# The reciprocal square roots of all norms, as one power on GpSimd in place of a root on ScalarE and a reciprocal on VectorE

## What is computed

```python
def _rmsnorm(x, g):
    xf = x.astype(jnp.float32)
    y = xf * lax.rsqrt(jnp.mean(xf * xf, axis=-1, keepdims=True) + NORM_EPS)
    return (y * g.astype(jnp.float32)).astype(x.dtype)
# layer one
h = _rmsnorm(x, p['ln_pre_a'][i]) * (1.0 + scale[:, None, :]) + shift[:, None, :]
...
x = x + gate[:, None, :] * _rmsnorm(y, p['ln_post_a'][i])
# between the layers and in layer two: the same two norms, and one per head
o = (_rmsnorm(o, p['subln_b'][j]) * (1.0 - lambda_init)).astype(x.dtype)
y = jnp.dot(o.reshape(b, t, DA_WIDTH) * jax.nn.silu(g), p['w_out_b'][j])
x = x + gate[:, None, :] * _rmsnorm(y, p['ln_post_b'][j])
```

## Time and profile before

| what | value |
|---|---|
| median of 3 runs | 1000.04 us |
| the runs | 1000.96, 994.45, 1000.04 us |
| span of the profiled execution | 1000.7 us |
| instructions in it | 15785 |
| busy: TensorE, VectorE, ScalarE, GpSimd | 914.8, 478.4, 414.2, 69.1 us |
| mean granted TensorE clock | 0.965 |

### The profile page before, as it was taken

One profiled execution on the slowest core, in us unless ns is written; L12 is line 12 of the kernel. 1 busy time (PEld: TensorE's weight loads), 2 busy tenths in 40 slices (PEclk: granted clock), 3 DMA queues, 4 the chain that ended last, 5 costly groups with the idle time before them and its releaser, 6 DMA issues.

```text
span 1000.7 us, 15785 instructions
## 1 busy us (share of the span) xinstructions
PE 914.8 (91%) x5704; PEld 700.9 (70%) x5704; DVE 478.4 (48%) x844; ACT 414.2 (41%) x889; POOL 69.1 (7%) x121
## 2 busy tenths in 40 slices
PE   2999999989999999889895899999989999888895
PEld 1576666767667777655684788888868888766784
DVE  0543232212277777466634824252366565456924
ACT  3421212102166656455626622242255555446623
POOL 0000000000111110021003000000010000110002
PEclk8799999989989999999898899999999999999999
DMA  9845654655410103197323122434201101488422
GB/s 340 322 166 187 233 196 142 209 212 189 126 43 22 42 21 126 57 328 258 137 84 134 38 101 74 180 108 145 64 22 43 40 23 43 149 296 268 171 85 105
DMA packets 71716, 138.35 MB, mean 138 GB/s; under 512 B 4592, under 2 KB 22256, under 8 KB 71536
## 3 DMA queue, kind: packets, MB, share of 16 engines
q1 hardware_dynamic: 68976, 127.15, 37.5%
q0 software_dynamic: 2688, 10.49, 2.7%
HBM read 121.37 MB, written 16.25 MB: 138 GB/s over the span
## 4 chain that ended last, share of the span: by engine, by line
PE 82%; DMA 5%; DVE 4%; ACT 4%; issue 3%; SPq 2%; POOL 0%; DVEq 0%; ACTq 0%
PE bank L1528 18%; PE bank L1530 18%; PE bank L1529 18%; PE bank L1831 3%; PE bank L1692 3%; PE bank L1587 3%; PE bank L1569 2%; PE bank L1743 2%; PE bank L1709 2%; PE bank L1700 2%; PE bank L1846 2%; DMA arena<-in_mod_w_a 2%; PE bank L1542 1%; PE bank L1754 1%; PE bank L1792 1%
## 5 line engine op out<-in xcount | busy, mean ns | idle before, releaser
L1528 PE MATMUL bank<-w_parts,h_parts 128*128 128x512 f32 x640 | 257.7, 403 | 7.2 <-DVE h_parts L1111 3.6
L1530 PE MATMUL bank<-w_parts,h_parts 128*128 128x512 f32 x640 | 251.7, 393 | 0.0
L1529 PE MATMUL bank<-w_parts,h_parts 128*128 128x512 f32 x640 | 251.4, 393 | 0.0
L719 ACT ACTIVATE w_parts<-arena 128x1024 fp32r<-128x1024 f32 x64 | 67.4, 1054 | 213.2 <-PE bank L1530 200.1
L1528 PEld LDWEIGHTS bank<-w_parts,h_parts 128*128 128x128 f32 x640 | 121.6, 190 | 44.5 <-issue 14.1
L1105 DVE TENSOR_TENSOR w_parts<-arena,w_parts 128x1024 fp32r<-128x1024 f32 x64 | 78.2, 1222 | 129.8 <-ACT w_parts L719 129.4
L1530 PEld LDWEIGHTS bank<-w_parts,h_parts 128*128 128x128 f32 x640 | 121.4, 190 | 26.4
L1529 PEld LDWEIGHTS bank<-w_parts,h_parts 128*128 128x128 f32 x640 | 121.7, 190 | 23.7
L1528 PE MATMUL bank<-h_parts,w_parts 128*128 128x320 f32 x256 | 90.0, 351 | 0.8 <-ACT arena L809 0.8
L1530 PE MATMUL bank<-h_parts,w_parts 128*128 128x320 f32 x256 | 79.4, 310 | 0.0
L1529 PE MATMUL bank<-h_parts,w_parts 128*128 128x320 f32 x256 | 79.3, 310 | 0.0
(11 more groups left out here) (159 smaller groups left out, 1237.6 us busy)
## 6 DMA issues: line engine op xcount, KB each, us to landing
arena<-in_w_in_a SPq DMA_DIRECT2D x32, 512.0 KB, 5.8
arena<-in_mod_w_b SPq DMA_DIRECT2D x24, 512.0 KB, 4.7
arena<-in_mod_w_a SPq DMA_DIRECT2D x4, 2048.0 KB, 15.6
arena<-in_mod_w_kv SPq DMA_DIRECT2D x16, 512.0 KB, 5.2
arena<-in_cache_a_k SPq DMA_DIRECT2D x8, 1024.0 KB, 7.0
arena<-in_cache_a_v SPq DMA_DIRECT2D x8, 1024.0 KB, 6.4
arena<-in_w_kv_b SPq DMA_DIRECT2D x16, 512.0 KB, 3.5
arena<-in_w_in_b SPq DMA_DIRECT2D x16, 512.0 KB, 3.8
```

Of the source, the lines that this page charges most:

```text
L719: nc.scalar.activation(whl[:, n % 2, 0, :], wraw[n % 2], ACT.Copy).then_inc(s_whi, 1)
L1528: mm(out, ah, wh, start=start, stop=False)
L1529: mm(out, ah, wl, start=False, stop=False)
L1530: return mm(out, al, wh, start=False, stop=stop)
```

## The change

One function `root` on GpSimd raises a variance to the power of -0.5 (`tensor_tensor` with `ALU.pow` against a tile `minus_half`, filled once at the start). It takes the place of ScalarE's Sqrt and VectorE's reciprocal at all 14 places: two of 128x5, ten of 128x1, one of 128x32, one of 128x8. The semaphores `sqrt_done` and `y_sqrt` are gone. GpSimd waits for the variance and signals "ready" itself. In the residual updates GpSimd's list is now root 0, root 1, addition 0, root 2, addition 1, and so on.

```diff
+        minus_half = sb("minus_half", [P, NT * PAIRS])
...
+            def root(dst, src, n):
+                return nc.gpsimd.tensor_tensor(dst, src, minus_half[:, 0:n], ALU.pow)
+
+            def norm_root(stage):
+                a, b = TT * stage, TT * (stage + 1)
+                pool.wait_ge(s_var, stage + 1)
+                root(rstd[:, a:b], ss[:, a:b], TT).then_inc(s_rstd, 1)
+                pool.wait_ge(s_rstd, stage + 1)
+
+            nc.gpsimd.memset(minus_half[:, :], -0.5).then_inc(s_half, 1)
+            pool.wait_ge(s_half, 1)
+            norm_root(0)
             store("ak", knat, 1)
...
                 for t in range(TT):
-                    pool.wait_ge(s_ys, layer * TT + t + 1)
-                    nc.gpsimd.tensor_tensor(x[:, t, 0:NC], x[:, t, 0:NC], ysb[:, t, 0:NC], ALU.add).then_inc(s_x2p, 1)
+                    pool.wait_ge(s_yv, layer * TT + t + 1)
+                    root(yvar[:, 0, t:t + 1], yvar[:, 1, t:t + 1], 1).then_inc(s_yr, 1)
+                    pool.wait_ge(s_yr, layer * TT + t + 1)
+                    if t == 0:
+                        continue
+                    add_y(layer, t - 1)
+                add_y(layer, NT)
                 pool.wait_ge(s_x2p, (layer + 1) * TT)
...
             residual(0)
+            norm_root(1)
...
+            pool.wait_ge(s_ov, 1)
+            root(osum[:, 0:NT * PAIRS], osum[:, 0:NT * PAIRS], NT * PAIRS).then_inc(s_osr, 1)
+            pool.wait_ge(s_ov, 2)
+            pool.wait_ge(s_osr, 1)
+            root(osum[:, NT * PAIRS:], osum[:, NT * PAIRS:], PAIRS).then_inc(s_osr, 1)
+            pool.wait_ge(s_osr, 2)
             residual(1)
...
-                act.wait_ge(s_var, stage + 1)
-                nc.scalar.activation(ss[:, TT * stage:TT * (stage + 1)], ss[:, TT * stage:TT * (stage + 1)],
-                                     ACT.Sqrt).then_inc(s_sqrt, 1)
...
-            def y_root(layer, t):
-                act.wait_ge(s_yv, layer * TT + t + 1)
-                nc.scalar.activation(yvar[:, 2, t:t + 1], yvar[:, 1, t:t + 1], ACT.Sqrt).then_inc(s_ysr, 1)
...
-            def head_root(columns, n):
-                act.wait_ge(s_ov, n)
-                nc.scalar.activation(osum[:, columns], osum[:, columns], ACT.Sqrt).then_inc(s_osr, 1)
...
-                dve.wait_ge(s_sqrt, stage + 1)
-                nc.vector.reciprocal(rstd[:, a:b], ss[:, a:b]).then_inc(s_rstd, 1)
...
-                dve.wait_ge(s_ysr, layer * TT + t + 1)
-                nc.vector.reciprocal(yvar[:, 0, t:t + 1], yvar[:, 2, t:t + 1]).then_inc(s_yr, 1)
...
-                link(nc.vector.reciprocal(osum[:, c], osum[:, c]))
```

## The result

The changed kernel took 1015.28 us (median of 4 runs, 1013.93 to 1016.77), beside 1000.5 us for the kernel before: a ratio of 1.0147, 95% interval 1.0109 to 1.0184. The forecast was 1000.9 with a range up to 1009. So the change costs 10 to 15 us. The places at which it acts lose 9.1 to 9.3 us in both traces of the changed kernel. What else the first set has stays open.

What follows compares the result with a forecast made beforehand. It took the kernel to be bound by TensorE's matmuls, which the change leaves alone. Gains of 2.4 us less 3.3 us of powers made a net loss of 0.9 on 1000.04: 1000.9 us, range 994 to 1009.

Steps and rivals of the forecast that it cites:

- the price of a power: Each GpSimd power: 0.2 us fixed plus 0.04 us a column, estimated from additions; 1.48 us for 128x32.
- 6 p1 + p5 + p32: Powers counted on the path, p1, p5, p32 being durations of 128x1, 128x5, 128x32 (0.24, 0.40, 1.48 us): 3.3 us.
- Rival (1): Power slow per column on GpSimd: chance 0.13 beyond 0.25 us a column (over 10 us), 0.04 from 0.1 to 0.25.
- 43 c - 0.8: Net loss in us if a power costs c us a column; passes 10 us from c = 0.25.
- Place A: First norm: comes 1.3 - p5 earlier, but TensorE's modulation and transposes cap the gain; 0.25 us taken.
- Place B: Residual update after `ya` and second norm: 1.1 - 3 p1 earlier at the square sums, 0.3 - p5 at the norm.
- Place C: Head norms: prompt 0.57 - p32 earlier; the samples' 128x8 power has 2.2 us and costs nothing.
- Place D: Last residual update, no table load there: 0.2 - 3 p1 earlier, a loss with any p1 above 0.07 us.
- Rival (2): First GpSimd power waits for code to load; a delay of 5 us gives 1005 us; chance 0.05.
- Rival (3): All removed loads, roots and reciprocals lie on the path: 6.8 us gained, 993 us; chance 0.03.
- The rule on table loads: ScalarE: the trace shows a 1.28 us load without the skill's further 1380 ns drain, which would add 1.4 us gain.
- Next to nothing lies around: Whole kernel: the profiled span of 1000.7 us was set 0.7 above the median of 1000.04.

Runs made afterwards that it cites:

- the first set: First four runs of the changed kernel beside the kernel before: median 1015.28 us, ratio 1.0147.
- delay: Kernel before with 13 chained small VectorE instructions, 2.7 us together, ahead of the second norm's variance: 1005.18 us, ratio 1.0033.
- best of both: Kernel before with the Sqrt table loaded ahead of the updates and the head norms' roots as split GpSimd powers: 1000.83 us, ratio 0.9991.
- price kernel: Kernel before with a row of powers and additions of several widths on scratch tiles while GpSimd is idle: 1001.09 us (one run).
- the second: Second set of four runs of the unaltered changed kernel, against the kernel before at 1001.23 us: 1010.8 us, ratio 1.0096.
- the repetition: Changed kernel, unaltered, run and traced again beside the kernel before: 1010.8 us, ratio 1.0096.

## Why the prediction was wrong, point by point

**What fails is the price of a power.** The step reads: "I take twenty additions, 0.04 us a column", on a fixed part of 0.2 us. Measured alone it is 0.157 us a column and 0.39 fixed. The term 6 p1 + p5 + p32 was put at 3.3 us. With the durations of the changed kernel's trace it is 6 x 0.99 + 1.18 + 5.46 = 12.6, and the same sum then gives a loss of 10.2 us in place of 0.9.

Of the 9.3 us between the two losses, 5.0 come from the slope, 1.5 from the fixed part and 2.7 from a third thing that the price left out: six of the powers stand in GpSimd's queue beside VectorE's updates and take 0.99 us, not the 0.55 of one alone. The slope was chosen between 0.002 and 1.3 without a row near it, from twenty steps of a routine; what the routine is, no run shows. The prediction named its own sign of being wrong, a 128x32 row above 5 us, and that came: 5.46.

That the sum with the right durations, 10.2, comes near the 9.1 to 9.3 of the traces is in part luck. It has the two updates 1.2 and 1.0 us too dear, and it lacks 1.0 us behind the second norm and the 0.25 at the first that never came. It has no term for the fall of the clock either. Rival (1) had the right mechanism, a routine per column. But its formula, 43 c - 0.8, gives 6 us at c = 0.157, since it has 0.2 us of fixed part for each of the eight powers, and the six of 128x1 take 0.99, not 0.36. The range ended at c = 0.25 on that formula, and so ended too low.

**Place A**: "It can save at most 1.90 - 1.64 = 0.26. Taken: 0.25, which holds while p5 is below 1.0." p5 was 1.18, and nothing was gained. Right by its own condition.

**Place B**: the 0.7 us at the first addition came about as predicted, 0.8 (3.23 against 4.06 us). "1.1 - 3 p1" would have been a loss of 1.9 with p1 = 0.99; measured 0.7. Two things made the difference. The additions were put at 1.43 us, but ahead of a power they take 1.26 to 1.29 (0.5 us for three). And the waits and gaps were put at 0.47 us, but one instruction follows the other in GpSimd's list within 0.02 us (0.4 us). That the longer mean of before holds time in which an addition waited for VectorE, which now falls on the powers, is a likely reading and not tested. The next norm's square sums, foretold 0.4 us earlier, start later. "0.3 - p5" gives a loss of 0.88; measured 0.86.

**An overlooked cover.** "Behind this norm's root on GpSimd are queued only the clears of `qz` and the stores of K and V, which nobody needs for a long time." Nobody needs them, but the root holds them back until VectorE scales. Then both slow down: 3.12 us for 2.08, 3.55 for 2.25. Between scaling and the store of K, the six traces with that overlap (the changed kernel twice, heads and updates put back, powers earlier, heads split) lose 0.98 to 1.77 us, 1.35 in the mean. The four without it (norms put back, clears moved, delay, best of both) lose 0.02 to 0.48, 0.30 in the mean. That is 1 us more.

**Place C**: "0.57 - p32" with 5.46 gives 4.89; measured 4.82, and 0.00 with the roots put back. For the samples, "The power of 128x8 has 2.2 us and costs nothing": it took 2.02 us, and VectorE waits for a head power only once, for the large one. Right.

**Place D**: "0.2 - 3 p1" gives a loss of 2.8; measured 1.7, for the same two reasons: the five additions take 6.8 us in place of 7.16, and the steps between 0.1 in place of 0.7.

**Rival (2)**, that the first power waits for code: it took 1.19 us, the second 1.18. In the price kernel the configuration instructions stand at 194.7 us and the first power starts at 194.85, with 0.56 us. Neither shows a delay. The slack of place A was put at 1.0 us; with p5 = 0.40 it is 0.9, and it holds the 0.25 that was already counted as gained. The 6 us that the Trainium skill has for a first call (GPSIMD Engine Reference, "Instruction dispatch") are not seen here. **Rival (3)** fell with the sum.

**The rule on table loads.** By the Trainium skill (ScalarE: Activation LUTs, "What ACT_TABLE_LOAD costs"), with its further 1380 ns of drain, place B would have been better by another 1.4 us. It isn't: the third square starts 1.36 us behind the second now (536.14 to 537.50), where it was 2.11, a gain of 0.75. Load and root together took 1.40 us (536.13 to 537.53), and the square now waits 0.67 us for TensorE in their place; that leaves no room for a drain.

**"Next to nothing lies around"** the span was wrong: the executions here take 1.75 to 1.87 us more than their spans (1016.77 against 1014.9; 997.66 against 995.9). The sum doesn't hang on it, since both kernels have it.

**What stays open.** Why the first set of the changed kernel has a median 4.5 us above the second. The one trace of it that there is shows 1.6 us by the granted clock at 744 us and 1.6 us more than the repetition up to the end of the samples; whether its other three runs had the same is not on record. Also open is why a delay brings the clock's fall, and why the repetition has none. A power on VectorE was not tried.

## What to carry over

Before work moves to another engine, its price there must come from a row of that operation on that engine; if none exists, let the range cover the worst price that the trace's bounds allow, because a power on GpSimd took 5.43 us where an addition of the same 32 columns took 0.25. A small instruction costs its place in the list: ask what it holds back and beside whom that will then run. Where a slow small operation must stay, split it so that the part whose input is ready early runs in idle time: 6.7 us of powers then cost nothing, where 5.5 us in one piece cost 4.8.

## What the hardware showed

- A power on GpSimd takes 0.55 us for 1 column, 1.01 for 4, 1.64 for 8, 2.90 for 16 and 5.43 for 32, the same on 32 partitions as on 128. ScalarE's root and VectorE's reciprocal took 0.2 and 0.17 us for 128x1, 0.23 and 0.35 for 128x32.
- The price depends on VectorE. A power of 128x1 behind an addition, with nothing on VectorE, took 0.55 to 0.56; behind an addition of 128x512 and beside VectorE's update L1135, which took 0.74 us alone and 1.65 to 1.86 there, it took 0.99. A power of 128x8 took 1.64 alone and 2.54 when it started just behind VectorE's product of two SBUF operands, which kept its 4.63 us. The Trainium skill (SBUF — State Buffer, "SBUF: two separate sides") says that such an operation of VectorE and a GpSimd one that reads SBUF hold a shared pair of ports in turn, each for a whole instruction. By that a product of 4.63/4 = 1.16 us would hold the power back by up to 1.1 us; the trace agrees with 0.90 (2.54 - 1.64). Two rows speak against the whole of the rule. In the price kernel VectorE's product of two SBUF operands (L1133) started at 207.22 us, in the middle of the power of 32 columns (203.85 to 209.28), and took its usual 1.23 us, as the power took its usual 5.43. And VectorE's further products went on beside the 2.54 us power. So a power under way held up no such operation of VectorE, and only its start seems to wait. That the ports are the cause was not tested apart.
- Clears on GpSimd beside VectorE's scaling: 3.55 and 3.12 us, apart 2.25 and 2.08.
- Behind two pauses of 0.9 and 1.0 us TensorE's granted clock fell to the level of 1.2 GHz in eight of the nine traces in which the way from the first update to 726 us is 1.9 us or more longer than before, and in none of the four others. It cost 1.6 us.
- The same kernel before, profiled twice, lay 5.6 us apart at 535 us. A difference of 1 us between kernels can't be read from spans here. From event to event in the traces it can over some 15 us: the six traces with the changed kernel's update lose 0.68 to 0.70 us there. Over the 70 us to the store of K, kernels with the same instructions differ by up to 0.8 us.
